# The first block's normalised row moves to PSUM, scores go to the second banks of the query stripes, and the ring for rows of table u has four places

## The reference, cut to what matters

```python
def peer_ffn(h, w_q, subkeys, u, v):
    q = (xt @ w_q).reshape(n, PEER_HEADS, 2, PEER_HALF)          # 8 heads, 2 lists
    s = jnp.einsum('nhpd,hpkd->nhpk', q, subkeys)                 # 128 keys in each list
    s_top, i_top = lax.top_k(s, PEER_TOPK)                        # 16 of each
    cand = s_top[:, :, 0, :, None] + s_top[:, :, 1, None, :]
    best, sel = lax.top_k(cand.reshape(...), PEER_TOPK)           # 16 experts a head, 128 a token
    gate = jax.nn.softmax(best, axis=-1)
    a = jax.nn.gelu(jnp.einsum('ted,td->te', u[ib], xb), approximate=False)
    return jnp.einsum('te,ted->td', gb * a, v[ib])                # u and v have 16384 rows of 2048
```

## Time and profile before

| | |
|---|---|
| median of three runs | 4494.3 us |
| the profiled execution, its own time | 4489.1 us |
| its span, first to last instruction | 4487.4 us |
| PE busy over the span | 4225.1 us (94%) |
| DVE busy | 2644.1 us (59%) |
| ACT busy | 1246.5 us (28%) |
| POOL busy | 1617.8 us (36%) |
| mean granted clock of TensorE, as a share of full speed | 0.967 |

### The profile page before, as it was taken

How to read it: one execution, slowest core, us unless ns; L and a number is a source line. 1 busy time by engine, 2 the same in 40 slices (tenths; PEclk the granted TensorE clock), 3 DMA queues, 4 the chain that set the end, 5 groups by cost and what they waited for, 6 DMA issues and landing times. The chain is left out here.

```text
span 4487.4 us, 76575 instructions
## 1 busy us (share of the span) xinstructions
PE 4225.1 (94%) x28752; PEld 4120.9 (92%) x28752; DVE 2644.1 (59%) x3611; ACT 1246.5 (28%) x1625; POOL 1617.8 (36%) x1260
## 2 busy tenths in 40 slices
PE   7999999999798899979999999988779999999997
PEld 6999999999565899979999999988779999999997
DVE  5222111111332542254888999996578888888887
ACT  4111133332222221133233233232223233333322
POOL 0000100000111000001467787787846655556662
PEclk9999999999798999989999999998889999999999
DMA  6722333333486443245778888888799999999996
GB/s 219 283 80 84 133 108 103 108 100 103 151 297 248 152 138 113 66 143 179 253 275 288 291 298 284 281 292 280 269 359 363 358 359 362 356 358 361 358 354 258
DMA packets 282481, 1061.64 MB, mean 237 GB/s; under 512 B 43762, under 2 KB 94322, under 8 KB 229170
## 3 DMA queue, kind: packets, MB, share of 16 engines
q1 hardware_dynamic: 165474, 521.67, 32.7%
q0 software_dynamic: 90256, 498.99, 30.3%
q10 hardware_dynamic: 26624, 39.37, 2.4%
HBM read 977.47 MB, written 81.33 MB: 236 GB/s over the span
## 5 line engine op out<-in xcount | busy, mean ns | idle before, releaser
L145 DVE TENSOR_TENSOR w_lo<-w_raw,w_hi 128x1024 fp32r<-128x1024 f32 x490 | 590.6, 1230 | 1000.1 <-ACT w_hi L136 998.4
L136 ACT ACTIVATE w_hi<-w_raw 128x1024 fp32r<-128x1024 f32 x490 | 509.9, 1058 | 1189.7 <-PE acc L173 728.7
L1469 POOL DMA_INDIRECT routes_scratch<-gate_sums,route x384 | 588.5, 1532 | 146.1 <-issue 114.9
L173 PE MATMUL acc<-x_hi,w_hi 128*128 128x288 f32 x2592 | 557.2, 297 | 9.8 <-DVE w_lo L145 9.2
L173 PE MATMUL acc<-x_lo,w_hi 128*128 128x288 f32 x2592 | 556.9, 297 | 0.3 <-issue 0.3
L173 PE MATMUL acc<-x_hi,w_lo 128*128 128x288 f32 x2592 | 556.2, 296 | 0.0
L173 PE MATMUL acc<-h_hi,w_hi_peeru 128*128 128x384 f32 (+1 forms) x1280 | 409.6, 336 | 42.1 <-DVE w_lo_peeru L145 42.1
L173 PEld LDWEIGHTS acc<-x_hi,w_hi 128*128 128x128 f32 x2592 | 419.2, 189 | 10.6 <-DVE w_lo L145 9.7
L173 PE MATMUL acc<-h_hi,w_hi 128*128 128x384 f32 (+1 forms) x1280 | 402.3, 331 | 25.8 <-DVE w_lo L145 25.8
L173 PEld LDWEIGHTS acc<-x_lo,w_hi 128*128 128x128 f32 x2592 | 419.4, 189 | 0.5 <-issue 0.5
L173 PEld LDWEIGHTS acc<-x_hi,w_lo 128*128 128x128 f32 x2592 | 419.2, 189 | 0.0
(11 more groups left out here) (332 smaller groups left out, 8273.5 us busy)
## 6 DMA issues: line engine op xcount, KB each, us to landing
w_raw<-in_w_peer_u SPq DMA_DIRECT2D x256, 512.0 KB
w_raw<-in_w_peer_v SPq DMA_DIRECT2D x256, 512.0 KB
w_raw<-in_w_gate SPq DMA_DIRECT2D x96, 512.0 KB, 3.7
w_raw<-in_w_z SPq DMA_DIRECT2D x66, 512.0 KB, 3.4
k_ring<-in_cache_k SPq DMA_DIRECT2D x64, 512.0 KB, 5.5
v_ring<-in_cache_v POOLq DMA_DIRECT2D x64, 512.0 KB, 7.1
routes_scratch<-zero POOLq DMA_DIRECT2D x8, 3072.0 KB, 46.0
activations_scratch<-a_out ACTq DMA_DIRECT2D x128, 192.0 KB
```

The source lines that it names most:

```text
L136: nc.scalar.activation(slot(q, j)[0], raw[:, j % 4, :], ACT.Copy).then_inc(q["hi"], 1)
L145: nc.vector.tensor_tensor(lo, raw[:, j % 4, :], hi.bitcast(F32), ALU.subtract).then_inc(q["lo"], 1)
L173: last = nc.tensor.matmul(dst, l_, r_[:, cc, c0:c0 + cn], start=(cc == first and p_ == 0), stop=(cc == last_c and p_ == 2))
L1469: pool.indirect_dma_start(route_dram, bass.IndirectOffsetOnAxis(ap=route[:, b, n:n + 1], axis=0), gsum[:, h % SUMS, b - 1, n % PTOP:n % PT ...
```

## The change

Three edits in the first PEER block. The row `h_row` of block 0, which every second and third dot reads, moves from SBUF to the four banks of `tps` in PSUM. The 24 KB ring takes over the 8 KB that this frees and has four places, used in turn by all gathers (`q % 4`), and gather q waits for dot q-4. Since `tps` is taken, the scores go to the second banks of `acc`, which u stripes leave free: token blocks 0 and 1, and 2 and 3, right after the third stripe of the group as before, and block 4 (the samples) after the fourth stripe, into the bank that blocks 0 and 1 used, once ScalarE has copied them. TensorE also waits for the three score copies of the head before when it begins a group.

```diff
-        ring = at("ring", [P, 3, D], F32, O_T)
-        hrow = at("h_row", [P, D], F32, O_T + 24576)
+        ROWS_IN = 4
+        ring = at("ring", [P, ROWS_IN, D], F32, O_T)
+        hrow = tps[:].rearrange("p a c -> p (a c)")
...
                 def gather(q):
                     i, r = divmod(q, 3)
-                    if q >= 3:
-                        pool.wait_ge(s_used, q - 2)
+                    if q >= ROWS_IN:
+                        pool.wait_ge(s_used, q - ROWS_IN + 1)
...
-                    pool.indirect_dma_start(ring[:, r, :], None, a["peer_u"], bass.IndirectOffsetOnAxis(ap=at_, axis=0)).then_inc(s_gat[r], 16)
+                    pool.indirect_dma_start(ring[:, q % ROWS_IN, :], None, a["peer_u"], bass.IndirectOffsetOnAxis(ap=at_, axis=0)).then_inc(s_gat[q % ROWS_IN], 16)
...
-                def copy_scores(h):
+                def copy_scores(h, groups):
...
-                        nc.scalar.activation(sc[:, 2 * g:2 * g + nb].rearrange("p b l k -> p (b l k)"), tps[:, g, 0:nb * 256],
+                        nc.scalar.activation(sc[:, 2 * g:2 * g + nb].rearrange("p b l k -> p (b l k)"), acc[:, g % 2, 1, 0:nb * 256],
...
                     if s % GROUP == 3 and s // GROUP < PH:
-                        copy_scores(s // GROUP)
+                        copy_scores(s // GROUP, (0, 1))
+                    if s % GROUP == 4 and s // GROUP < PH:
+                        copy_scores(s // GROUP, (2,))
...
                 def dot(q):
                     i, r = divmod(q, 3)
-                    dve.wait_ge(s_gat[r], 16 * i + 16)
+                    k = q % ROWS_IN
+                    dve.wait_ge(s_gat[k], 16 * (q // ROWS_IN + 1))
                     c = 2 * i + r if r < 2 else NEXP + i
-                    nc.vector.scalar_tensor_tensor(out=ring[:, r, :], in0=ring[:, r, :], scalar=1.0, in1=hrow[:] if r < 2 else hrow_s[:],
+                    nc.vector.scalar_tensor_tensor(out=ring[:, k, :], in0=ring[:, k, :], scalar=1.0, in1=hrow if r < 2 else hrow_s[:],
...
-                def scores(h):
-                    pe.wait_ge(q6["act"], GROUP * h + 4)
-                    pe.wait_ge(s_skl[h % 2], 16 * (h // 2 + 1))
-                    if h:
-                        pe.wait_ge(s_cop, 3 * h)
-                    for b in range(NBLK):
+                def scores(h, blocks):
+                    if blocks[0] == 0:
+                        pe.wait_ge(q6["act"], GROUP * h + 4)
+                        pe.wait_ge(s_skl[h % 2], 16 * (h // 2 + 1))
+                    else:
+                        pe.wait_ge(s_cop, 3 * h + 1)
+                    for b in blocks:
...
-                            last = nc.tensor.matmul(tps[:, b // 2, c0:c0 + NKEY], qp[:, p, b * P:(b + 1) * P], sk[:, h % 2, p, :],
+                            last = nc.tensor.matmul(acc[:, b // 2 % 2, 1, c0:c0 + NKEY], qp[:, p, b * P:(b + 1) * P], sk[:, h % 2, p, :],
...
                 for g in range(PH):
+                    if g:
+                        pe.wait_ge(s_cop, 3 * g)
                     for r in range(3):
                         one(GROUP * g + r)
-                    scores(g)
+                    scores(g, (0, 1, 2, 3))
                     one(GROUP * g + 3)
+                    scores(g, (4,))
```

More of the change, by code:

```diff
@@ L1389, in build @@
         s_st = [sem(f"activations_stored{k}") for k in range(2)]
-        s_gat = [sem(f"u_row_gathered{k}") for k in range(3)]
+        s_gat = [sem(f"u_row_gathered{k}") for k in range(ROWS_IN)]
         s_used, s_sct, s_gel = sem("u_row_used"), sem("gates_scattered"), sem("gelu_done")
@@ L1517, in copy_scores @@
                         act.wait_ge(s_lst, NBLK * h)
-                    for g in range(3):
+                    for g in groups:
                         nb = min(2, NBLK - 2 * g)
                         act.wait_ge(s_sco, 3 * h + g + 1)
-                        nc.scalar.activation(sc[:, 2 * g:2 * g + nb].rearrange("p b l k -> p (b l k)"), tps[:, g, 0:nb * 256],
+                        nc.scalar.activation(sc[:, 2 * g:2 * g + nb].rearrange("p b l k -> p (b l k)"), acc[:, g % 2, 1, 0:nb * 256],
                                              ACT.Copy).then_inc(s_cop, 1)
@@ L1685, in _ @@
                     if s == 0:
-                        nc.vector.scalar_tensor_tensor(out=hrow[:], in0=x1[:, 0, :], scalar=rstd2[:, 0:1], in1=g_row[:],
+                        nc.vector.scalar_tensor_tensor(out=hrow, in0=x1[:, 0, :], scalar=rstd2[:, 0:1], in1=g_row[:],
                                                        op0=ALU.mult, op1=ALU.mult).then_inc(s_hr, 1)
```

## The result

The changed kernel takes 4448.64 us (median of 4 runs, 4443.31 to 4451.35) beside 4493.13 us of the kernel before (4 runs, 4486.68 to 4501.08): ratio 0.9895, 95% interval 0.9876 to 0.9914. It is faster, as forecast, but by 44.5 us between these medians where 33 were forecast. So the gain was 38 to 51 us, and each way of reading it lies above 33: 38.1 between the profiled executions, 44.5 between the medians, 50.5 in the second measurement, against its own chip's 4491.75.

What follows compares the result with a forecast made beforehand. GpSimd was taken as the bound from 3040 to 3266 us, held up by dots with two SBUF sources. Savings of 31 us there and 2 us from 3266 to 3352 gave 4494.3 - 33 = 4461 us, range 4448 to 4483.

Steps and rivals of the forecast that it cites:

- (a): 3040 to 3266 us: with h_row in PSUM its dots stop holding GpSimd up, taking 33 us off GpSimd's time.
- (b): Entry to the 3040 to 3266 us stretch: four ring places put GpSimd one gather further ahead, 5 us (0 to 6).
- (c): 3040 to 3266 us: DMA engines limit next at 189 us, GpSimd at 188; stretch put at 195, 31 us saved.
- (d): 3266 to 3352 us, scatters over: a fourth place removes most GpSimd waits, but DMA engines limit; 2 us (0 to 3).
- (e): 2300 to 2980 us and before: TensorE hides GpSimd's gain, and a PSUM source costs VectorE nothing; 0.
- (g): At 1958 us: h_row's one write goes to PSUM beside the first stripe's matmuls; 0.
- (f): Moved scores: TensorE's new wait for score copies is over before it is reached; 0, bounded by -1 and +2 us.
- DMA takes it back: Rival: with scatters queued, DMA engines land gathers later; gain about 12 us, 4482 us; chance 0.12.
- No effect of PSUM: Rival: dots hold GpSimd up as before, only the fourth place acts; say 4489 us; chance 0.08.
- Slower: Rival: dots read four PSUM banks slower, VectorE bounds 2300 to 2980 us; about 4563 us; chance 0.03.

Runs made afterwards that it cites:

- the second measurement: The unmodified changed kernel measured once more on another chip, against the kernel before on that chip: 4441.27 us, ratio 0.9885.

## Why the prediction was right and where it was off

The mechanism held: the operands decide whether a dot holds GpSimd up, and GpSimd bounded the stretch. The signs named for "right" came: dots at 2280 ns, indirect DMAs within them at 0.97 us, GpSimd's mean 1.24 us (1.25 was named), the last scatter 39 us earlier (30 was named), no idle time at the scores' matmuls, the dots at 3008.00 and 3026.23 at their old places. One missed narrowly: a DMA share of 0.92, not 0.93 or more. Step by step:

(a) *33 us less of GpSimd's time, bounds 30 to 35.* From 1.52 to 1.24 us over 113 DMAs is 32 us, and the course became 27.8 us shorter; 33 x 113/121 = 31 was the forecast for it. The rest went into a longer wait for a scatter's landing (6.9 against 5.4 us) and into waits for dots that GpSimd did not have before (3.7 us in four places). Right in kind, some 3 us too high in effect.

(b) *Four places, 5 us, from 0 to 6.* Measured 11.0 (places alone), and 11.5 together with the row in PSUM, which alone gives 6.3. This term was sized by GpSimd's own round of 5.9 us, as if GpSimd were the only clock at the entry. But around the sums it is not; POOL in order of time, kernel after, where the earlier trace rows has it before:

```profile
3013.91 2.29 POOL L1482 DMA_INDIRECT ring<-in_peer_u,eidx  x1 [0.30 <-issue]
...
3028.80 1.72 POOL L1482 DMA_INDIRECT ring<-in_peer_u,expert_sample  x1 [10.03 <-DVE ring L1684]
...
3036.61 1.72 POOL L1482 DMA_INDIRECT ring<-in_peer_u,eidx  x1 [2.80 <-DVE ring L1684]
3042.47 0.98 POOL L1482 DMA_INDIRECT ring<-in_peer_u,eidx  x1 [0.30 <-issue]
```

GpSimd now stands 10.03 us in front of the sums where it stood 2.01: it comes there 8 us ahead, which the prediction valued at nothing because TensorE hides everything before 2980 us. What is saved under cover is not lost when it can be carried as a lead to the place where the cover ends. The number of places caps that lead, for the gather at 3028.80 waits for the dot behind the sums. VectorE in order of time, kernel after:

```profile
3008.00 2.28 DVE L1684 SCALAR_TENSOR_TENSOR ring<-ring,tps 128x2048 f32<-128x2048 f32 x1
...
3026.23 2.29 DVE L1684 SCALAR_TENSOR_TENSOR ring<-ring,tps 128x2048 f32<-128x2048 f32 x1
```

A place is therefore worth a spacing of VectorE's dots, 18.2 us here and 7.8 us at the next release (3036.61 - 3028.80), and not only a round of 5.9. The earlier trace rows had GpSimd waiting for dots at both places: there the dots were the clock. How the 11.5 us split between the two parts is not known better than this, since the parts overlap (11.0 and 6.3 alone). That the lead is what the places bring is read from this trace; no run varies it by itself.

(c) *The DMA engines next: 189 us, and 195 for two limits that don't overlap.* This step failed, and with (b) it makes the miss. The share of 0.97 was read as a ceiling because it was the highest in sight. The run without scatters holds 1.02 over 110 us, and with half the bytes the course takes 180.0 us, where with all of them it takes 181.9 and 179.4. What filled the course after the change was GpSimd still: 138.6 us busy, 32.6 between one instruction and the next, 6.9 for a landing and 3.7 for dots, together the 181.9. The prediction put GpSimd alone at 188 of the 226 us. 226 less the measured 11.5 and 27.8 is 187, so the 7 us added for the DMA engines were never there. The lower end of the range, built on a share of 1.00 and a gain of 46, was no bound either. A share that a stretch shows tells what was asked of the engines in it; a ceiling is shown only where something waits for them.

(d) *3266 to 3352, 2 us:* 1.5 measured between the marks, less than two executions differ by. The run with half the bytes bears out its reason, that there the transfers hold the dots up. (e), (g) *0:* 4141 matmuls at 2300 to 2980 against 4144. A dot against four PSUM banks takes 2280 ns (2265 to 2289), some 10 ns less than the 2291 of the earlier trace rows. The Trainium skill ("VectorE: DVE Perf Modes", section on the TRN2 errata) would have each some 65 ns longer; the trace does not agree. (f) *0:* the scores alone 0.999.

The sum: 33 + 5 - 7 + 2 = 33 us forecast, 27.8 + 11.5 + 0 + 1.5 = 40.8 measured between the marks, 38.1 between the profiled executions. The failed (c) accounts for 7 us of the difference, the undersized (b) for 6.5, and (a) took 5 back.

The rivals: "DMA takes it back" had a gain of 12 and a share under 0.9; the result is 44.5 and 0.92, and half the bytes change nothing in the course. "No effect of PSUM" is what the kernel with the row in SBUF does, at 4478 where 4489 was priced: again (b) undersized, 7 us with (d) then, and 13 measured between the last dots (1355.4 and 1342.0). "Slower" needed 0.75 us more for a dot and got none.

The Trainium skill ("SBUF — State Buffer", section "Who interferes with whom") is borne out as far as two SBUF sources against one go, now at full length of a dot: 3.05 us and 0.97 us within 6 us of the same trace.

## What to carry to other kernels

Ask of every two-source VectorE instruction of some length, while GpSimd issues DMAs, whether one source can lie in PSUM: here it took 0.28 us, in the mean, off 113 indirect DMAs for no price on VectorE. Taking the last such instructions away brought nothing more here. When an engine becomes faster, write the order anew that was made for its old speed; the block's end came another 11 to 16 us earlier. A saving under cover is worth what of it can be carried, as a lead, to the end of the cover, and the number of buffers caps the lead.

## What was not expected of the hardware

The DMA engines moved 420 GB/s at a share of 1.02 for 110 us, where the highest row before was 387 GB/s. An indirect DMA of 128 rows that no dot holds takes GpSimd mostly 0.97 to 0.99 us, whether the rows have 2048 elements, 1024 or one. And TensorE can stand still again and again, up to 1.6 us at a time, with no engine or transfer named, its granted clock at 0.50 for a while; in the kernel with all dots in PSUM this took back the 20 us that TensorE no longer waited for `w_lo`. Its cause was not found.
